# A block form of seven products for gate and up in the feed-forward layers of a two-block transformer kernel

## What is computed

```python
def swiglu_2(h, w1, w3, w2):
    return (jax.nn.silu(h @ w1) * (h @ w3)) @ w2
...
y = swiglu(rms_norm(x, g[4]), ffn_wg[layer], ffn_wu[layer], ffn_wd[layer])
x = x + rms_norm(y, g[5])
...
x = x + 0.5 * swiglu_2(rms_norm_2(x, ffn1_norm[l]), ffn1_w1[l], ffn1_w3[l], ffn1_w2[l])
...
x = x + 0.5 * swiglu_2(rms_norm_2(x, ffn2_norm[l]), ffn2_w1[l], ffn2_w3[l], ffn2_w2[l])
```

## Time and profile before

| | us |
|---|---|
| median of 3 runs | 2107.32 |
| lowest and highest of them | 2105.61 and 2108.77 |
| span of the profiled execution, first to last instruction | 2102.9 |

### The profile page before, as it was taken

How to read it: one execution, slowest core, us unless ns; L and a number is a source line. 1 busy time by engine, 2 the same in 40 slices (tenths; PEclk the granted TensorE clock), 3 DMA queues, 4 the chain that set the end, 5 groups by cost and what they waited for, 6 DMA issues and landing times.

```text
span 2102.9 us, 26995 instructions
## 1 busy us (share of the span) xinstructions
PE 2028.6 (96%) x9980; PEld 1673.4 (80%) x9980; DVE 1253.8 (60%) x1890; ACT 1045.6 (50%) x1698; POOL 140.9 (7%) x146
## 2 busy tenths in 40 slices
PE   7988899999889999999999999999999999999999
PEld 6875688887768888888778788888888877888887
DVE  5646755567764556455767865556455675865544
ACT  5644644355664445445456645435444556555343
POOL 0000100000000000000402200000000312120000
PEclk9987999999999999999999999999999999999999
DMA  7530466554335555555552545655555653435552
GB/s 273 156 116 12 142 197 192 188 190 141 99 122 181 194 185 180 182 195 168 153 192 77 180 160 181 192 188 180 183 196 182 184 170 121 152 129 179 192 181 99
DMA packets 247145, 346.13 MB, mean 165 GB/s; under 512 B 26148, under 2 KB 180072, under 8 KB 247016
## 3 DMA queue, kind: packets, MB, share of 16 engines
q1 hardware_dynamic: 245768, 342.65, 50.4%
q0 software_dynamic: 544, 1.29, 0.3%
q10 hardware_dynamic: 704, 0.48, 0.1%
HBM read 343.32 MB, written 2.33 MB: 164 GB/s over the span
## 4 chain that ended last, share of the span: by engine, by line
PE 89%; DVE 4%; ACT 2%; issue 2%; POOL 1%; DMA 1%; SPq 0%; ACTq 0%; DVEq 0%; POOLq 0%
PE bank L697 26%; PE bank L699 26%; PE bank L698 26%; PE bank L973 2%; PE bank L1293 1%; PE bank L1101 1%; PE bank L632 1%; ACT w_hi L529 1%; PE bank L1433 1%; POOL gain L2698 1%; PE bank L1151 1%; DVE w_lo L511 1%; PE bank L2104 1%; DMA raw<-in_ev_w_in 1%; DVE jobstat L1020 0%
## 5 line engine op out<-in xcount | busy, mean ns | idle before, releaser
L511 DVE TENSOR_TENSOR w_lo<-raw,w_hi 128x2048 fp32r<-128x2048 f32 (+6 forms) x505 | 739.7, 1485 | 416.1 <-ACT w_hi L529 415.8
L697 PE MATMUL bank<-w_hi,h_hi 128*128 128x512 f32 (+3 forms) x1872 | 739.8, 395 | 15.3 <-issue 5.1
L529 ACT CAST w_hi<-raw 128x2048 fp32r<-128x2048 f32 (+6 forms) x505 | 618.1, 1253 | 263.0 <-PE bank L699 259.9
L698 PE MATMUL bank<-w_lo,h_hi 128*128 128x512 f32 (+3 forms) x1904 | 733.6, 385 | 0.0
L699 PE MATMUL bank<-w_hi,h_lo 128*128 128x512 f32 (+3 forms) x1872 | 725.0, 387 | 0.0
L697 PEld LDWEIGHTS bank<-w_hi,h_hi 128*128 128x128 f32 x1872 | 356.0, 190 | 87.6 <-issue 7.8
L698 PEld LDWEIGHTS bank<-w_lo,h_hi 128*128 128x128 f32 x1904 | 362.7, 190 | 63.8
L699 PEld LDWEIGHTS bank<-w_hi,h_lo 128*128 128x128 f32 x1872 | 355.5, 190 | 69.6
L697 PE MATMUL bank<-w_hi,ff_hi 128*128 128x512 f32 x528 | 206.3, 391 | 0.0
L699 PE MATMUL bank<-w_hi,ff_lo 128*128 128x512 f32 x528 | 205.6, 389 | 0.0
L698 PE MATMUL bank<-w_lo,ff_hi 128*128 128x512 f32 x528 | 205.5, 389 | 0.0
(11 more groups left out here) (326 smaller groups left out, 1680.5 us busy)
## 6 DMA issues: line engine op xcount, KB each, us to landing
raw<-in_ffn_w SPq DMA_DIRECT2D x176, 512.0 KB, 4.7
raw<-in_w_in SPq DMA_DIRECT2D x48, 1024.0 KB, 5.3
raw<-in_ffn_w SPq DMA_DIRECT2D x44, 1024.0 KB, 4.9
raw<-in_ffn_wg SPq DMA_DIRECT2D x44, 512.0 KB, 4.0
raw<-in_ffn_wu SPq DMA_DIRECT2D x44, 512.0 KB, 5.0
raw<-in_ffn_wd SPq DMA_DIRECT2D x22, 1024.0 KB, 4.9
raw<-in_od_w_in SPq DMA_DIRECT2D x12, 1024.0 KB, 5.1
raw<-in_w_out SPq DMA_DIRECT2D x8, 1024.0 KB, 5.0
```

The source lines that it names most:

```text
L511: dve.tensor_tensor(lo_[:, cs], raw_[:, cs], hi[:, cs].bitcast(F32), ALU.subtract).then_inc(*dve_did.up())
L529: act.copy(hi[:, cs], raw_[:, cs]).then_inc(*act_did.up())
L697: pe.matmul(out, x_hi, u.hi[:, k, cols_], start=start, stop=False)
L698: pe.matmul(out, x_hi, u.lo[:, k, cols_], start=False, stop=False)
```

## The change

In each feed-forward layer the chunks (4, 5) and (8, 9) are computed as pairs (`FAST_PAIRS`). The gate and up product of a pair is a product of a 2 x 2 block matrix of the inputs (token tile by half of the inputs: a11, a12, a21, a22) and a 2 x 2 block matrix of the weights (half of the inputs by chunk: b11, b12, b21, b22). The plain form has eight block products; the new one is the known form with seven (Strassen and Winograd), with these sums:

- inputs: s1 = a21 + a22, s2 = s1 - a11, s3 = a11 - a21, s4 = a12 - s2
- weights: t1 = b12 - b11, t3 = b22 - b12, t2 = t3 + b11, t4 = b21 - t2 (`weight_sum`, VectorE)
- products (`product`, 12 matmuls each): a11 b11, s1 t1, s2 t2, a12 b21, s3 t3, a22 t4, s4 b22

Products that share a term accumulate in one bank; `keep` copies the state between them to SBUF on ScalarE, and `joined` adds the parts on VectorE, takes the silu and multiplies.

The seven weight operands b11, t1, t2, b21, t3, t4, b22 are each split in high and low, in two pieces of 1024 (`pieces_n = 2`). t1, t2 and t4 stand in three areas that are free during the layer (`extra`), t3 in the place of b12. Since the sums need raw weights, b11 and b22 are split only after t2 has been computed, and b21 only after t4. Loading order (`loads`) and order of use (`units`) are no longer the same: a slot waits for its own predecessor (`slot_before`), and t3 gives b12's slot free.

The inputs are needed with their norm factor. Once for each layer, in chunk 1, two small matmuls spread the factors over the partitions and VectorE forms `hn` (two instructions of 128x2048). In chunk 2 VectorE forms the sums (`mix_tokens`), ScalarE rounds them, and VectorE takes the low parts (`split_tokens`).

The down products of chunk 3 (7) stand inside the pair, and those of 4 and 5 (8 and 9) in the chunk behind it, with the transposes of both.

```diff
+FAST_PAIRS = (4, 8)
...
+    while c < chunks:
+        if c in FAST_PAIRS:
+            b11, b21, b12, b22 = [gate_up(c + m, k0) for m in range(2) for k0 in (0, KD // 2)]
+            t1, t2, t3, t4 = [Unit(b11.shape, None) for _ in range(4)]
+            for u in (b11, b21, b22, t1, t2, t3, t4):
+                u.summed, u.pieces_n = False, 2
+            sevens[c] = Seven(b11, b12, b21, b22, t1, t2, t3, t4)
+            before = down(c - 1)
+            loads += [b11, b12, b22, b21, before]
+            takes += [b11, t1, t2, b21, before, t3, t4, b22]
...
             def _(sp):
-                if i >= RAW_SLOTS:
-                    sp.wait_ge(*units[i - RAW_SLOTS].used)
+                if u.slot_before is not None:
+                    sp.wait_ge(*u.slot_before.used)
...
                     dve.wait_ge(*rounded)
+                    if u.last_sum is not None:
+                        dve.wait_ge(*u.last_sum)
...
             u = split_units[n]
+            if not u.summed:
+                return False
...
+                    dve.tensor_tensor(hn[:, :, :], h_hi[:, :, :].bitcast(F32), h_lo[:, :, :].bitcast(F32),
+                                      ALU.add).then_inc(*dve_did.up())
...
+                    dve.tensor_tensor(hn[:, :, :], hn[:, :, :],
+                                      bank.t[:, 0:T].unsqueeze(1).broadcast_to([P, KD, T]),
+                                      ALU.mult).then_inc(*dve_did.up())
...
+            def middle_sums(g):
+
+                weight_sum(g.t3, g.b22, g.b12, ALU.subtract, g.b22.landed)
+                weight_sum(g.t2, g.t3, g.b11, ALU.add, g.t3.landed)
...
+            def fast_pair(c, g):
+
+                (a_, f_), (e_, d_) = pair[c % 2], pair[(c + 1) % 2]
+                take()
+                product("a11", g.b11, a_, [a_.drained])
+                s1 = keep(0, a_)
+                take()
+                product("s1", g.t1, d_, [d_.drained])
+                fifth = pe_did.now()
+                transposes(c - 1)
+                take()
+                product("s2", g.t2, a_, [s1], False)
+                s16 = keep(1, a_)
+                take()
+                product("a12", g.b21, f_, [f_.drained])
+                f_.drained, multiply = joined(c, 0, 0, 0, s1, f_, pe_did.now())
+                down(c - 1, take())
+                multiply()
+                take()
+                product("s3", g.t3, a_, [s16], False)
+                g.b12.used = g.t3.used
+                s167 = keep(2, a_)
+                a_.drained = s167
+                fifth_read, multiply = joined(c + 1, 1, 2, 3, s167, d_, fifth)
+                take()
+                product("a22", g.t4, e_, [e_.drained])
+                multiply()
+                e_.drained, multiply = joined(c, 1, 2, 2, s167, e_, pe_did.now())
+                take()
+                product("s4", g.b22, d_, [fifth_read], False)
+                multiply()
+                d_.drained, multiply = joined(c + 1, 0, 1, 1, s16, d_, pe_did.now())
+                multiply()
...
-            for c in range(1, NF + 1):
-                if c < NF:
-                    gate_up(c, take(), 0)
-                if 1 <= c < NF:
-                    transposes(c - 1)
-                if c < NF:
-                    gate_up(c, take(), KD // 2)
-                    hidden(c)
...
+            while c < NF:
+                if c in FAST_PAIRS:
+                    fast_pair(c, seven[c])
+                    c += 2
+                    continue
+                follows = c - 2 in FAST_PAIRS
+                g = seven.get(c + 1)
+                gate_up(c, take(), 0)
+                if c == 1:
+                    token_scales()
+                if g is not None:
+                    first_sum(g)
+                transposes(c - 2 if follows else c - 1, pair[(c + 1) % 2][1] if follows else None)
+                if c == 2:
+                    mix_tokens()
+                if g is not None:
+                    middle_sums(g)
+                gate_up(c, take(), KD // 2)
+                if g is not None:
+                    last_sum(g)
+                hidden(c)
+                if c == 2:
+                    split_tokens()
+                if follows:
+                    transposes(c - 1, pair[(c + 1) % 2][0])
+                    down(c - 2, take())
```

More of the change, by code:

```diff
@@ L297, in half_units @@
     return gemm_units(W[k0 * P:(k0 + KD // 2) * P, :], chunked(D))
+Seven = namedtuple("Seven", "b11 b12 b21 b22 t1 t2 t3 t4")
 def ffn_units(wg, wu, wd):
-    units = []
     chunks = wd.shape[0] // FF_CHUNK
[L304 to L313, removed]
@@ new lines, in ffn_units @@
+    loads, takes, sevens, owed, c = [], [], {}, [], 0
+    while c < chunks:
[8 more added lines that the diff above has]
+            takes += [b11, t1, t2, b21, before, t3, t4, b22]
+            owed = [c, c + 1]
+            c += 2
+            continue
+        both = [gate_up(c, 0), gate_up(c, KD // 2)]
+        both += [down(m) for m in owed]
+        loads += both
+        takes += both
+        owed = [] if c + 1 in FAST_PAIRS else [c]
+        c += 1
@@ L320, in weight_stream, with flush, feed_forward @@
+    both = [down(m) for m in owed]
+    return loads + both, takes + both, sevens
+def weight_stream(a):
+    loads, takes, sevens, units = [], [], [], []
+    def flush():
+        loads.extend(units)
+        takes.extend(units)
+        units.clear()
+    def feed_forward(*w):
+        flush()
+        first, second, third = ffn_units(*w)
+        loads.extend(first)
+        takes.extend(second)
+        sevens.append(third)
     for l in range(DEPTH):
@@ new lines, in place_sums, with weight_sum, _ @@
+            def place_sums(g):
+                for u, m in ((g.t1, 0), (g.t2, 1), (g.t4, 2)):
+                    u.raw, u.lo = (v[:, :].rearrange("p (a b) -> p a b", a=u.shape[0]) for v in (extra[m], extra_lo[m]))
+                g.t3.raw, g.t3.lo = g.b12.raw, g.b12.lo
+            def weight_sum(u, one, other, op, *landed):
+                @block.vector
+                def _(dve):
+                    for mark in landed:
+                        dve.wait_ge(*mark)
+                    dve.tensor_tensor(u.raw, one.raw, other.raw, op).then_inc(*dve_did.up())
+                u.landed = dve_did.now()
@@ new lines, in last_sum, with product, _ @@
+            def last_sum(g):
+                weight_sum(g.t4, g.b21, g.t2, ALU.subtract, g.b21.landed, g.t2.landed)
+                for u in (g.b21, g.t2, g.t4):
+                    u.summed, u.last_sum = True, dve_did.now()
+            MIXED = {"s1": 0, "s2": 1, "s3": 2, "s4": 3, "a11": 4, "a12": 5, "a22": 6}
+            def product(name, u, bank, waits, first=True):
+                m = MIXED[name]
+                lo = mixed_last[:, :, :] if m == 6 else mixed_lo[:, m, :, :]
+                @block.tensor
+                def _(pe):
+                    pe.wait_ge(*mixing["split"])
+                    for mark in waits:
+                        pe.wait_ge(*mark)
+                    pe.wait_ge(*u.parted)
+                    for k in range(KD // 2):
+                        hi, low = mixed_hi[:, m, k, :], lo[:, k, :]
+                        begin, end = first and k == 0, k == KD // 2 - 1
+                        pe.matmul(bank.t[:, :], hi, u.hi[:, k, :], start=begin, stop=False, skip_group_check=True)
+                        pe.matmul(bank.t[:, :], hi, u.lo[:, k, :], start=False, stop=False, skip_group_check=True)
+                        mm = pe.matmul(bank.t[:, :], low, u.hi[:, k, :], start=False, stop=end, skip_group_check=True)
+                    mm.then_inc(*pe_did.up())
+                u.used = pe_did.now()
```

156 lines of the change are left out of this document (142 added, 14 removed).

## The result

The changed kernel takes 2133.4 us (median of 4 runs, 2130.8 to 2135.2), against 2106.5 for the one before (2105.6 to 2108.8): 1.0129 times as long, with a 95% interval of 1.0114 to 1.0143. The profiled execution of after has a span of 2133.3 us, against 2102.9, and took 2135.18 in all, so 1.9 us lie around its span.

What follows compares the result with a forecast made beforehand. TensorE was taken to bound the kernel. Six layers, each losing 8.45 us and winning 5.44, add 18 us: span 2102.9 becomes 2120.9, plus 4.4 around it gives 2125.4 us. Forecast range 2111 to 2143 (0.63); 8-in-10 range 2092 to 2148.

Steps and rivals of the forecast that it cites:

- the layer's sum: Each feed-forward layer: 8.45 us lost in waits against 5.44 won, so 3.0 us more; 18 us in six layers.
- Twelve matmuls a pair: Gate and up products: 84 matmuls in place of 96, 2.72 us won a pair, 32.6 us over 12 pairs.
- The queue ahead of the first pair: VectorE from chunk 2 to t1's split: 26.3 us without a gap, ending at 40.1; TensorE loses 3.9 us.
- The stand-ins: VectorE's new weight sums and additions, absent from the earlier trace, were priced by instructions of the same shape elsewhere.
- The second pair's 0.1: From chunk 7: t1's split ends at 19.55 us, TensorE wants it at 19.53, a wait of 0.1 us.
- Behind a pair: After each pair TensorE waits 0.85 us ahead of chunk 6 or 10, then 1.05 us at the transposes.
- Chunk 1, 0.65: Chunk 1: small matmuls cost 0.3 us and `hn` holds `ff_lo` back on VectorE, 0.65 us lost in all.
- the condition that I had named as proof against the sum: A granted clock under 1.00 in these stages would prove the sum wrong, every matmul being priced at full clock.
- The first: VectorE keeps up in the queue to t1 and behind each pair: 2079, or 2102 with the later waits; chance 0.17.
- The second: It comes out even: half of the waits hold (25 us) against 32.6 won and 3.9 lost, 2104; chance 0.12.
- The third, late transfers: d(5), g(7,0) and g(7,1), requested together, land late: 36 us more, 2161; chance 0.08.
- The rule beside it: VectorE instructions never overlap their predecessor: the long queue ends 1.4 us later, 9 us in six layers, 2134.

Runs made afterwards that it cites:

- both orders: Changed kernel with the silu behind ScalarE's next cast and t4's sum behind t1's low parts on VectorE: 2102.0 us, 0.9986 of the kernel before.

## Why the prediction came out as it did

The forecast was 2125.4 us, 18 above the median of before; the time is 2133.4, 27 above, and inside the stated range of 2111 to 2143. The direction, the places of the waits and their kind were right, and what was off is the size of the layer's sum: 3.0 us predicted, 4.0 measured, in two layers 5.5 and 5.7. By its steps:

- **Twelve matmuls a pair, 5.44 us a layer: right**, 5.4 to 5.5 when done alone.
- **The queue ahead of the first pair: right to 0.2 us.** Start 13.8 into chunk 2, both; length 26.3 against 26.5. Waits 0.5, 0.9 and 2.5 us against 0.5, 1.0 and 2.4 (the distance from the start ahead, less 0.227: 2008.73 - 2006.09 - 0.23 = 2.41 for t1). The stand-ins held: a sum of 128x2048 takes 2.28 us, an addition in `joined` 0.68.
- **The second pair's 0.1: 0.26.** Behind a pair 0.85 and 1.05: 0.85 and 0.8. These too within the error of the walk.
- **Chunk 1, 0.65: too small**, 1.2 measured. The two calls that spread the factors are four matmuls in the trace, and take 0.44 us, not 0.3; that is also why the page shows 120 instructions of TensorE less and not the 132 that I had named. `ff_lo` comes 0.63 us late, not 0.35.
- **Left out: what a restart costs.** After a wait the first matmuls start 0.31 and 0.24 us apart and a few more 0.005 to 0.01 too far; by the twelfth it is 0.12 us. A layer has nine waits, three of them at transposes or right behind them, where most of such a loss stood already. With the waits it makes 6.05 us for the first pair, where I had 5.8, and 2.25 for the second, where I had 2.0. Chunk 1's 0.55 and 0.25 for each pair close the gap between 3.0 and 4.0.
- **The clock: the condition that I had named as proof against the sum came true.** Every matmul was priced at full clock; behind the wait for t1 it fell to a mean of 0.66 over 5 us, in two of six layers, 1.6 us each. That the idle time causes it is shown by all kernels together: with a wait of 2.3 us the clock fell in 9 of 18 layers, with one of 1.2 us in none of 18, with the wait filled in none of 6. Why it falls in one layer and not in another is not shown.
- **Around and outside the layers.** 3.2 us of the span lie outside the layers. Two waits for a low part of 1.4 and 1.1 us stand there, at the two places shown above, which the kernel before doesn't have; why they come is open, and the sum had nothing for it. Between other kernels, whose edits don't touch these stages, they differ as much: from 1.4 us less than in before to 5.8 more. The median rose by 3.5 us less than the span did, for 1.9 us lie around a span and not the 4.4 that I had taken. By that the profiled execution of before took 2104.8 us, so it was one of its quicker ones.

**The rivals.** The first, that VectorE keeps up, gave 2079 with chunk 1's loss alone. It did not happen here, but the same instructions in another order give 2077.6. My argument against it, that no instruction could be left out of the queue, was true and beside the point: its start waited for a cast that only stood ahead of it on ScalarE, and one of its sums stood in it too early. The wait for t1 was not a lack of VectorE's time. The second, that half of the waits hold, did not come: all came at about the size of the walk. The third, late transfers, is not in the trace: no new wait of TensorE leads to a DMA.

**The rule beside it.** By the sentence of the Trainium skill that the prediction took ("VectorE: DVE Perf Modes", section "The DRAIN you can't avoid") the queue would have been 1.4 us longer, 27.7; it was 26.5, and two waiting-free low parts took 4.49 us again. I had left out the end of the same paragraph, by which a next instruction that is not held starts earlier. With it the section and the rows agree, and the rule was no rival. The time of 2134 that it gave lies near the measured 2133 for another reason.

## What to carry to other kernels

Ask first whether an engine is late because it has too much to do or because of what it does first: here 27 us came from two moved instructions and 56 us in all from moving a cast, a multiplication, a sum and a silu behind the work that TensorE wanted next, with no instruction less. In a fixed order, walk each queue and mark every instruction whose result is wanted later than that of the one behind it. A wait of TensorE has to be priced with its restart and, where it is as long as the 2.4 us of here, with the chance that the clock falls behind it.

## What the runs showed of the hardware that I had not expected

- **The clock behind a wait.** After the wait of 2.3 us for t1 (2.4 from start to start) the clock was 1.00 in four layers of after and 0.66, over 5 us, in two; with the silu behind the cast it fell in one layer of six, in the kernel with the mixing alone on GpSimd in all six. After the waits of 2.1 us near the start of a layer, in the two kernels with GpSimd, it fell in 3 of 8. After waits of 1.2 us it fell in none of 18 layers. So the same wait costs 2.4 or 4.0 us, and I can't tell from the program which.
- **GpSimd beside VectorE.** GpSimd needs 4.62 us for an addition of 128x2048 that VectorE does in 2.28, and VectorE's 2.29 us subtraction that starts beside it lasts 5.5 to 5.7. The 9.3 us of work in a layer that were moved to GpSimd brought nothing with both orders, and without them made the kernel 6.5 us slower than after.
- **A restart of TensorE** costs 0.12 us beside the wait itself, counted up to the twelfth matmul behind it.
